# Dense gates ahead of activations, no meetings at the stage ends, and the gates made inside the first stage's last two items

## The reference, cut to what matters

```python
def peer_ffn(h, w_pq, sub_keys_1, sub_keys_2, w_u, w_v):
    q = (hf @ w_pq).reshape(T, PEER_HEADS, 2, PEER_HALF)
    s1 = einsum('thd,kd->thk', q[:, :, 0], sub_keys_1)
    s2 = einsum('thd,kd->thk', q[:, :, 1], sub_keys_2)
    v1, i1 = lax.top_k(s1, 16)
    v2, i2 = lax.top_k(s2, 16)
    cand = (v1[..., :, None] + v2[..., None, :]).reshape(T, 8, 256)
    sc, ci = lax.top_k(cand, 16)
    experts = e1 * 128 + e2           # e1, e2: i1, i2 at ci // 16, ci % 16
    gates = softmax(sc)
    a = einsum('td,tkd->tk', hb, w_u[experts])
    return einsum('tk,tkd->td', gates * gelu(a), w_v[experts])
```

## Time and profile before

| | us |
|---|---|
| median of 3 runs | 3191.1 |
| lowest, highest | 3190.98, 3193.24 |
| the profiled execution's own time | 3190.46 |
| its span, first to last instruction | 3188.7 |
| PE busy in the span | 3054.4 (96%) |
| DVE busy | 2111.0 (66%) |
| ACT busy | 1369.0 (43%) |
| mean granted clock of PE | 0.985 of 2.4 GHz |

### The profile page before, as it was taken

The page is one execution under the profiler, slowest core; times in us unless marked ns, Lnnn a source line. Parts: engine busy times, 40 slices in busy tenths (PEclk is TensorE's granted clock), DMA queues, the critical chain, the costliest instruction groups (busy, mean ns, idle before and its releaser), DMA issues. The chain is left out here.

```text
span 3188.7 us, 47064 instructions
## 1 busy us (share of the span) xinstructions
PE 3054.4 (96%) x18562; PEld 2613.7 (82%) x18562; DVE 2111.0 (66%) x2725; ACT 1369.0 (43%) x1523; POOL 5.3 (0%) x8
## 2 busy tenths in 40 slices
PE   7999889899998999999999899999999999999998
PEld 6878777788876888787899888888888888877887
DVE  4646775656676545655578888645886468888745
ACT  4544454444434443445444444443333433344434
POOL 0000000000000000000000000000000000000000
PEclk9999999999998999999999999999999999999999
DMA  6555534245452455344444544455445554444553
GB/s 247 183 186 185 177 125 167 80 162 181 157 184 97 172 179 197 132 180 140 152 164 175 182 140 165 170 189 193 164 165 174 195 185 165 164 158 159 192 191 144
DMA packets 84985, 535.48 MB, mean 168 GB/s; under 512 B 9992, under 2 KB 13696, under 8 KB 27264
## 3 DMA queue, kind: packets, MB, share of 16 engines
q1 hardware_dynamic: 77248, 522.03, 46.9%
q10 hardware_dynamic: 7616, 11.78, 1.1%
HBM read 530.57 MB, written 3.15 MB: 167 GB/s over the span
## 5 line engine op out<-in xcount | busy, mean ns | idle before, releaser
L2074 DVE TENSOR_TENSOR w_lo<-raw,w_hi 128x2048 fp32r<-128x2048 f32 (+2 forms) x500 | 1130.1, 2261 | 907.4 <-ACT w_hi L1387 902.8
L1387 ACT ACTIVATE w_hi<-raw 128x2048 fp32r<-128x2048 f32 (+2 forms) x500 | 944.9, 1890 | 1094.7 <-PE ps L767 413.5
L765 PE MATMUL ps<-w_hi,hT 128*128 128x512 f32 (+3 forms) x1344 | 523.2, 389 | 28.3 <-DVE w_lo L2074 27.7
L767 PE MATMUL ps<-w_hi,hT 128*128 128x512 f32 (+3 forms) x1344 | 514.9, 383 | 0.0
L766 PE MATMUL ps<-w_lo,hT 128*128 128x512 f32 (+3 forms) x1344 | 514.8, 383 | 0.0
L1226 PE MATMUL ps<-hT,w_hi 128*128 128x512 f32 x1536 | 492.3, 402 | 1.6 <-DVEq L2914 0.8
L1230 PEld LDWEIGHTS ps<-hT,w_lo 128*128 128x128 f32 x1536 | 289.6, 189 | 68.5
L765 PEld LDWEIGHTS ps<-w_hi,hT 128*128 128x128 f32 x1344 | 255.3, 190 | 79.7 <-DVE w_lo L2074 23.5
L1266 PE MATMUL ps<-w_hi,c_hi 128*128 128x512 f32 x768 | 299.6, 390 | 3.8 <-DVE c_lo L2957 3.8
L1230 PE MATMUL ps<-hT,w_lo 128*128 128x256 f32 x1536 | 302.8, 279 | 0.0
L1268 PE MATMUL ps<-w_hi,c_lo 128*128 128x512 f32 x768 | 299.5, 390 | 0.0
(11 more groups left out here) (280 smaller groups left out, 4114.3 us busy)
## 6 DMA issues: line engine op xcount, KB each, us to landing
raw<-in_w_u_t SPq DMA_DIRECT2D x128, 1024.0 KB, 4.7
raw<-in_w_v SPq DMA_DIRECT2D x128, 1024.0 KB, 5.3
raw<-in_w_in_2.0 SPq DMA_DIRECT2D x32, 1024.0 KB, 4.7
raw<-in_odd_w.0 SPq DMA_DIRECT2D x20, 1024.0 KB, 4.7
raw<-in_even_w.3608 SPq DMA_DIRECT2D x16, 1024.0 KB, 4.9
raw<-in_w_out.0 SPq DMA_DIRECT2D x16, 1024.0 KB, 4.9
raw<-in_w_out.1 SPq DMA_DIRECT2D x16, 1024.0 KB, 4.9
raw<-in_w_out_2.0 SPq DMA_DIRECT2D x16, 1024.0 KB, 4.7
```

Of the source, the lines that this page charges most:

```text
L765: pe.matmul(o, hi, wh, start=(j + k == 0), stop=False)
L767: mm = pe.matmul(o, lo, wh, start=False, stop=(j == 3 and k == 3))
L1387: act.activation(w_hi[:, s % 2, 0:size], raw[:, s, 0:size], ACT.Copy).then_inc(hi_done, 1)
L2074: dve.tensor_tensor(w_lo[:, s % 2, 0:size], raw[:, s, 0:size], w_hi[:, s % 2, 0:size].bitcast(F32), ALU.subtract).then_inc(lo_done, 1)
```

## The change

- On PE the dense step of an item stands ahead of its activations, in U1, U2 and U3. DVE's step turns with it: sum, weigh, one-hot rows of the item after next, split; so `hots(0)` and `hots(1)` both stand ahead of the loop.
- The meetings at the ends of U1, U2 and U3 are gone. In the last step of a U stage DVE weighs first, makes the `c_lo` of the coming V stage's first item and sums last; ACT makes that item's `c_hi` ahead of the last gelu. The first V item goes through banks 4 to 7 first and waits for the last sum and weighing ahead of banks 0 to 3; in V2 such waits stand ahead of banks 2 and 3 and ahead of the first dense gates.
- In U0 the choosing is laid into 30 items (`SPARE` 3.45). Two `pair` calls take the place of the meetings: the Exp stands on ACT ahead of item 30's gelu, the sums and quotients on DVE after the split in item 30, and the split in item 31 moves behind the turn of the keys.
- A Sqrt that warms its table stands ahead of the last squares of the norm before the expert layer.

```diff
@@ outputs, half_outputs (PE)
-            for b in range(8):
+            for b in (4, 5, 6, 7, 0, 1, 2, 3) if first and q < HALVED else range(8):
+                if first and q < HALVED and b == 0:
+                    pe.wait_ge(sums_done, QTR * (q + 1) + 2)
+                    pe.wait_ge(gate_used, STEPS * (q + 1) + 2)
...
+                    if first and k == 0:
+                        pe.wait_ge(sums_done, QTR * (HALVED + 1) + 2)
                     dense(i + 4 * k, s, PARTS - 1, 2 * k)
...
+                    if first and k + j + t == 0:
+                        pe.wait_ge(gate_used, STEPS * (HALVED + 1) + 2)
@@ after U0 (PE)
-        st.meet()
-        st.meet()
-        st.meet()
+        st.take()
         turn(plan["keys"])
         pe.drain().then_inc(gate_ready, 2)
-        st.meet()
         with pe.Fori(0, LOOPS) as i:
             for s in range(RAW):
+                dense(i, s, 0)
                 activations(i, s, 1)
-                dense(i, s, 0)
-        st.meet()
...
                     for s in range(RAW):
+                        dense(i, s, q + 1)
                         activations(i, s, q + 2)
-                        dense(i, s, q + 1)
-                st.meet()
@@ norm (ACT)
+        act.activation(sm(144), sm(145), ACT.Sqrt)
         squared(3)
@@ u_part (ACT)
             for s in range(RAW):
+                if q == 0 and s == RAW - 2:
+                    st.pair()
+                    act.activation(SC16, SC16, ACT.Exp)
                 if s < RAW - 1 or q == 0:
                     u_split(LOOPS - 1, s, q)
+                if s == RAW - 1 and q > 0:
+                    act.wait_ge(gate_used, STEPS * q + 2)
+                    if q - 1 == HALVED:
+                        half_high(0, 0, 0, 0)
+                    else:
+                        high(0, 0, q - 1)
                 activate(LOOPS - 1, s, q)
+                if q == 0 and s == RAW - 2:
+                    st.pair()
@@ U0 (DVE)
-        SPARE = 3.3
+        SPARE = 3.45
...
-        for n in range(QTR):
+        for n in range(QTR - 2):
             u_split(n // 4, n % 4, 0)
             while spent < SPARE * (n + 1):
                 spent += next(choosing, SPARE)
         for _ in choosing:
             pass
-        st.meet()
-        st.meet()
+        st.pair()
+        u_split(LOOPS - 1, RAW - 2, 0)
+        st.pair()
         for t in range(NT):
...
-        st.meet()
+        st.hand()
+        dve.drain().then_inc(sums_done, 1)
         turn(plan["keys"])
         dve.drain().then_inc(gate_used, 2)
-        st.meet()
+        u_split(LOOPS - 1, RAW - 1, 0)
+        st.pair()
@@ weave (DVE)
-                more = not (last and s == RAW - 1)
-                if more:
-                    hots(i + (s + 1) // RAW, (s + 1) % RAW, g)
-                    u_split(i, s, q)
-                elif g == HALVED:
-                    hots(0, 0, g + 1)
+                if last and s == RAW - 1:
+                    weigh(i, s, g)
+                    if g == HALVED:
+                        half_low(0, 0, 0, 0)
+                        hots(0, 0, g + 1)
+                    else:
+                        low_c(0, 0, g)
+                    add_halves(i, s, q)
+                    return
                 add_halves(i, s, q)
                 weigh(i, s, g)
+                if not last or s < RAW - 2:
+                    hots(i + (s + 2) // RAW, (s + 2) % RAW, g)
+                u_split(i, s, q)
 
             hots(0, 0, g)
+            hots(0, 1, g)
```

More of the change, by code:

```diff
@@ L1948, in u_split @@
             split(i + (u_first[q] // 4 + (s + 2) // 4), (s + 2) % 4, 2048)
-        def u_part(q):
-            with act.Fori(0, LOOPS - 1) as i:
-                for s in range(RAW):
-                    u_split(i, s, q)
[L1954 to L1959, removed]
         def high(i, s, q):
@@ L1966, in high @@
                            ACT.Copy).then_inc(c_hi_done, 1)
-        LOOPS = QTR // RAW
-        settle()
-        u_part(0)
-        st.meet()
-        act.activation(SC16, SC16, ACT.Exp)
-        st.meet()
-        st.meet()
-        turn(plan["keys"])
-        st.meet()
-        u_part(1)
-        st.meet()
         def half_high(i, s, k, j):
@@ L1986, in half_high, with u_part @@
                            ACT.Copy).then_inc(c_hi_done, 1)
+        def u_part(q):
+            with act.Fori(0, LOOPS - 1) as i:
+                for s in range(RAW):
+                    u_split(i, s, q)
+                    activate(i, s, q)
+            for s in range(RAW):
+                if q == 0 and s == RAW - 2:
+                    st.pair()
+                    act.activation(SC16, SC16, ACT.Exp)
+                if s < RAW - 1 or q == 0:
+                    u_split(LOOPS - 1, s, q)
+                if s == RAW - 1 and q > 0:
[4 more added lines that the diff above has]
+                        high(0, 0, q - 1)
+                activate(LOOPS - 1, s, q)
+                if q == 0 and s == RAW - 2:
+                    st.pair()
+        LOOPS = QTR // RAW
+        settle()
+        u_part(0)
+        turn(plan["keys"])
+        st.pair()
+        u_part(1)
         def half_step(i, s, k, end=False):
@@ L2004, in _ @@
             if q == HALVED:
-                half_high(0, 0, 0, 0)
                 for k in range(2):
@@ L2016, in _ @@
                 act.wait_ge(c_used, QTR)
-            high(0, 0, q)
             if q > HALVED:
+                high(0, 0, q)
                 split(v_first[q] // 4, 1, 2048)
@@ L2893, in add_halves, with half_low, low_c @@
                               ps[:, s % 2, :].rearrange("p (n t) -> p t n", n=2), AX, ALU.add).then_inc(sums_done, 1)
+        def half_low(i, s, k, j):
+            dve.wait_ge(c_hi_done, 8 * i + (c_first[HALVED] + 32 * k + 2 * s + j + 1))
+            dve.tensor_tensor(c_lo[:, j], CTS[HALVED % 2][:, bass.ds(8 * i + (2 * s + j), 1)].rearrange("p a t -> p (a t)"),
+                              c_hi[:, j].bitcast(F32), ALU.subtract).then_inc(c_lo_done, 1)
+        def low_c(i, s, q):
+            dve.wait_ge(c_hi_done, 4 * i + (c_first[q] + s + 1))
+            dve.tensor_tensor(c_lo[:, s % 2], CTS[q % 2][:, bass.ds(4 * i + s, 1)].rearrange("p a t -> p (a t)"),
+                              c_hi[:, s % 2].bitcast(F32), ALU.subtract).then_inc(c_lo_done, 1)
         def weave(q, g):
             def step(i, s, last=False):
-                more = not (last and s == RAW - 1)
-                if more:
-                    hots(i + (s + 1) // RAW, (s + 1) % RAW, g)
-                    u_split(i, s, q)
-                elif g == HALVED:
-                    hots(0, 0, g + 1)
+                if last and s == RAW - 1:
[7 more added lines that the diff above has]
+                    return
                 add_halves(i, s, q)
                 weigh(i, s, g)
+                if not last or s < RAW - 2:
+                    hots(i + (s + 2) // RAW, (s + 2) % RAW, g)
+                u_split(i, s, q)
             hots(0, 0, g)
+            hots(0, 1, g)
             with dve.Fori(0, LOOPS - 1) as i:
@@ L2912, in weave @@
                 step(LOOPS - 1, s, True)
-        dve.drain().then_inc(sums_done, 2)
+        dve.drain().then_inc(sums_done, 1)
         dve.tensor_copy(IOTA_B, IOTA)
@@ L2923, in _ @@
         weave(1, 0)
[L2924 to L2929, removed]
         def half_step(i, s, k, end=False):
@@ L2953, in _ @@
         for q in range(PARTS):
[L2954 to L2958, removed]
             def v_step(i, s, last):
                 if not (last and s == 3):
-                    low_c(i + (s + 1) // 4, (s + 1) % 4)
+                    low_c(i + (s + 1) // 4, (s + 1) % 4, q)
                 if not (last and (s >= 2 and q == PARTS - 1 or s == 3)):
@@ L2966, in _ @@
             if q == HALVED:
-                half_low(0, 0, 0, 0)
                 for k in range(2):
@@ L2977, in _ @@
                 continue
-            low_c(0, 0)
+            if q > HALVED:
+                low_c(0, 0, q)
             if q < HALVED:
```

## The result

| | before | after |
|---|---|---|
| median (13 runs each, same chip), us | 3191.1 | 3199.51 |
| lowest, highest | 3189.34, 3193.52 | 3196.55, 3202.32 |
| the profiled execution's own time | 3190.46 | 3198.18 |
| its span | 3188.7 | 3196.4 |

The ratio is 1.0026, with a 95% interval of 1.0018 to 1.0033: slower by 8.4 us. The forecast was 3202.4, 2.9 us too slow, with 3196.5 to 3207.5 as range.

A forecast was written before the change was run, and what follows sets the result against it. PE, busy 3054.4 of 3188.7 us, was taken as the bound, with only stage seams to win or lose. 16.5 - 3.0 - 1.5 - 2.3 + 1.0 + 0.6 = +11.3 us gave 3202.4 us, range 3196.5 to 3207.5.

The forecast's parts named there:

- The seams V to U: V0 to U2 and V1 to U3: PE's dense(0) waits for DVE's one-hot rows; +8.3 us each, together +16.5.
- The clock's part: At each V to U seam, PE restarts at a lowered clock after 6.7 us idle: 2.4 us lost, bounds 0 and 3.4.
- The seams U to V: U1 to V0, U2 to V1, U3 to V2: removed meetings save PE's waits; -3.0, -1.5 and -2.3 us.
- The residue of 0.3 us: At V0 and V1, the second V item's inputs take about 5.8 us against one V item of 5.45.
- the 2.3 forecast in V2: At U3 to V2, DVE's queued hots(0) and hots(1) make gelu, c_hi, c_lo and the second item's w_lo late: +2.3 us.
- The seam U0 to U1: Keys turn earlier, but PE's dense(0) then waits for DVE's rows: +1.0 us, 0 to +2.5; Exp table loads cost nothing.
- U0: Within U0, choosing packed into 30 items makes PE wait longer for w_lo: +0.6 us, 0 to +1.9.
- nothing which changes the order inside an item can gain: Mid-stage PE has no idle time worth naming, so only seams between stages can win or lose.
- (a): Rival, faster: PE finds rows ready at U2 and U3, the 16.5 fall away; -5.2 us, 3185.9; 5%.
- (b): Rival, no measurable change: holds without a clock fall, no residue paid at U3 to V2; +4.2, 3195.3; 10%.
- (c): Rival, much slower: later clock recovery after three holds, U0's waits doubled, U to V seams gain 1.5 less; 3208.2; 8%.
- The Sqrt's table: Loaded ahead of the last squares, which are themselves awaited on that path: 0 us, -1.2 to +0.3.

The follow-up runs named there:

- experiment 3: Kernel before with dense gates ahead of activations and DVE's step turned with them, all meetings and U0 kept: 3209.88 us, ratio 1.0055.
- experiment 1: Changed kernel, but DVE makes the coming stage's first one-hot rows, hots(0), early within V0 and V1: 3188.75 us, ratio 0.999 to the kernel before.
- experiment 5: Changed kernel with PE's loops in U1, U2 and U3 rotated so that a round ends behind the dense gates: 3205.95 us, ratio 1.0044 to the kernel before.
- Experiment 2: Kernel before with SPARE 3.45 instead of 3.3, nothing else: 3193.74 us, ratio 1.001.
- experiment 4: Changed kernel, but at V to U seams the first one-hot rows are made ahead of the second item's w_lo: 3194.34 us, ratio 1.0005 to the kernel before.
- experiment 6: Changed kernel with first rows made within V0 and V1, banks 0 and 1 emptied earlier, U1's first item doing activations first: 3178.20 us, ratio 0.996 to kernel before.

## Why the prediction was right, and where it was off

**The seams V to U, +16.5 forecast, +15.1 measured.** The mechanism is the one forecast, to the instruction: dense(0) waits for `hots(0)`, which DVE makes behind the second item's w_lo. PE starts 6.35 us later (6.71 - 0.36) and the first dense gates no longer wait their 0.52; twice that is 11.7 against the forecast's 11.6; experiment 3 gives the 6.71 with the turned loop alone, and experiment 1 takes it away by moving the rows alone. The clock's part was forecast as 2.4 at each and came out as 1.2 and 2.2; its size was taken from U0 to U1, where the changed kernel again loses 2.15 (first interval 8.42). The six holds of 6.71 and 6.87 us in the changed kernel and experiments 3 and 5 lose 1.2 to 2.4. So the one row that the forecast had gave the upper end, and the spread stated, 1.5 to 3.4, should have begun at 1.2.

**The seams U to V, -6.8 forecast, -6.4 measured.** Gap and V stage together: U1 to V0 -1.8 - 1.1 = -2.9 (forecast -3.0), U2 to V1 -1.8 + 0.5 = -1.3 (-1.5), U3 to V2 -3.0 + 0.8 = -2.2 (-2.3). The residue of 0.3 us forecast at V0 and V1 stands in the trace as a wait of 0.33 for c_lo. Of the 2.3 forecast in V2 the following wait is the larger part (PE's timeline), for a c_lo behind a w_lo of 2.28 us that starts at 2813.84; the other is 0.24 at 2811.64:

```profile
2816.61 0.47 PE L1298 MATMUL ps<-w_hi,c_hi 128*128 128x512 f32 x1 [1.93 <-DVE c_lo L2908]
```

The forecast had it from counting DVE's queue behind the seam instruction by instruction, the moved rows included.

**The seam U0 to U1, +1.0 forecast, +0.3 measured** (+0.6 up to the first product, -0.3 of clock in the first item). The sum for the first rows was 10.0 us behind U0's end (1834.6 - 1824.6) and they let PE start 9.6 behind it. Of the Exp and its tables nothing is on the path: ACT is through with the gelu at 1825.32, and DVE with its w_lo at 1826.02. ACT's timeline in item 30:

```profile
1823.64 1.28 ACT L1948 ACT_TABLE_LOAD   x1
1824.94 0.38 ACT L1948 ACTIVATE work<-ps 128x256 f32<-128x256 f32 x1
```

The load ends at 1824.92 and the next instruction starts 0.02 us later, as it did in the earlier trace rows; the 0.7 us that a drain would have added to this term is not there. The Trainium skill (ScalarE: Activation LUTs, What ACT_TABLE_LOAD costs) has 1380 ns for that drain; here the trace disagrees with it, and decides.

**U0, +0.6 forecast, +2.9 measured: the step that failed.** Its bound was 1.9, called a doubling of the waits, and even that was passed. It is the term that was mis-sized. Its cause, w_lo late between denser pieces, is the one forecast; two sizes in it were not. The waits themselves went from 1.8 us in three places to 3.8 in six, 2.0 more, where 0.6 was taken from the shape of one collision. And a stop costs more than its wait. The view of PE around one of them:

```profile
1652.62 0.28 PE L1240 MATMUL ps<-hT,w_lo 128*128 128x256 f32 x1
1653.66 0.38 PE L1238 MATMUL ps<-hT,w_hi 128*128 128x256 f32 x1 [0.76 <-DVE w_lo L2081]
1653.88 0.28 PE L1239 MATMUL ps<-hT,w_hi 128*128 128x256 f32 x1
```

Products follow each other every 0.12 us; here two steps take 1.04 + 0.22 = 1.26, so the stop is 1.02 us for a wait of 0.76. Three more stops at 0.26 on top of their waits are 0.8 us, 2.8 together. Experiment 2 shows that this is the whole term and due to the one constant.

**Not foreseen: the turn of the loop, -3.4.** That nothing which changes the order inside an item can gain was wrong. The rows that say so were there in the kernel before: the starts of the dense gates are 6.27 us apart three times and 6.43 the fourth. The mean of 6.33 hid it. Experiment 5 gives it back.

**The sum.** Forecast 16.5 - 6.8 + 1.0 + 0.6 = 11.3; measured 15.1 - 6.4 + 0.3 + 2.9 - 3.4 = 8.5, against 7.7 between the profiled executions, from which these terms are read, and 8.4 between the medians. The 0.8 us left over lie in no term. The two large misses, +2.3 and -3.4, have opposite signs. That the sum came nearer than its terms is luck.

**The rivals.** (a), rows ready at U2 and U3, is out by the 6.71. (b), holds without a fall of the clock, is out by the 0.50 in both. Of (c) one part came true, U0's doubled waits. The clock fell anew behind each of the three holds, but it did not come back later than forecast, and the U to V seams gave what was forecast to within 0.4 us. The Sqrt's table was about 0 as forecast: it is loaded at 1522.67, earlier by 1.95 us than in the earlier trace rows, and the Sqrt behind the squares starts at 1525.88 instead of 1525.92.

## What to carry to other kernels

When a step is moved to the front of a stage on an in-order queue, look up what stands ahead of its *inputs* on the queue that makes them: here a w_lo of 2.29 us and rows of 2.3 us, for which PE had waited 0.5 us, became 6.7 us of hold, twice, and the clock fell with them. The cure is to make the first inputs of the next stage within the one that runs, at a place where neither queue has a due item behind them; against the changed kernel that was worth some 16 us at the two seams V to U. At U1, whose rows come from the choosing that has just ended, the step that needs no rows goes first, once: that was worth 5 us more. In U0 a stop cost its wait and 0.26 us for the restart, with products 0.12 us apart. A mean over items hides what happens once per round of a loop.

## What was new about the hardware

- The turn of a loop on PE cost 0.15 to 0.21 us (once 0.28) behind 24 products of 32 columns (kernel before, experiment 5), and nothing that shows behind the activations with their products of 256 and 512 columns (6.27 us at each turn of the changed kernel).
- From U0 on, in all nine profiles, the clock was down behind every gap of PE of 2.38 us and more (2.38, 2.97, 3.67, 5.73 and longer). Of ten gaps of 1.77 to 1.96 us it was down behind four: in the kernel before it is 0.57 in 2040 to 2044, after 1.78 us idle, and 1.00 in 2420.6 to 2424 after 1.77. V2's wait of 1.93 to 1.96 is nearly the same in the kernels without the meetings. Behind it the clock stays in the changed one (1.93) and falls in experiments 5 and 4 (both 1.96; by stretch, in this order), and in experiment 1 it stays at 1.00 after 1.96. So the length of the gap doesn't decide it; what does is open.

```profile
2816.00:2820.00 4.00, 3.39 (x34) 1.00 0.57 171
```

```profile
2824.00:2828.00 4.00, 3.55 (x10) 0.67 0.61 209
```

```profile
2813.00:2817.00 4.00, 3.74 (x10) 0.63 0.67 197
```

- "issue" as the releaser can be a wait on another engine. The 0.52 in the earlier trace rows was one, for DVE's rows, and the 0.44 at 2217.32 in experiment 6 is another: the last instruction of `hots(1)` ends at 2217.21, 0.11 us earlier.
